# First block's mixers: the fourth scan output and the gate products of RWKV stand ahead of GLA's levels 5 and 6 on TensorE, not behind them

## Reference

```
# GLA: gated linear attention with a decay per key column (4 heads, key 32, value 64)
scores[i, j] = sum_k q[i, k] * k[j, k] * exp(cum[i, k] - cum[j, k])     for j <= i
out = scores @ v + (q * exp(cum)) @ state
out = rms_norm(out) * silu(gate)

# RWKV7 (4 heads of 64), token by token
sa    = -state @ kk
state = state * w + sa (kk * a)^T + v k^T
out   = state @ r
y     = (group_norm(out) + bonus) * (sigmoid(g_lr) @ g2)
```

## Time and profile before

| | us |
|---|---|
| median of 3 runs | 2974.25 |
| lowest and highest | 2971.95, 2977.4 |
| the profiled execution, its own time | 2977.13 |
| its span, first to last instruction | 2975.3 |
| PE busy in the span | 2775.5 (93%) |
| DVE busy | 1543.2 (52%) |
| ACT busy | 1086.0 (37%) |
| mean granted clock of PE | 0.952 |

### The profile page before, as it was taken

How to read it: one execution, slowest core, us unless ns; L and a number is a source line. 1 busy time by engine, 2 the same in 40 slices (tenths; PEclk the granted TensorE clock), 3 DMA queues, 4 the chain that set the end, 5 groups by cost and what they waited for, 6 DMA issues and landing times. The chain is left out here.

```text
span 2975.3 us, 38798 instructions
## 1 busy us (share of the span) xinstructions
PE 2775.5 (93%) x14972; PEld 2386.3 (80%) x14972; DVE 1543.2 (52%) x2136; ACT 1086.0 (37%) x1524; POOL 208.2 (7%) x205
## 2 busy tenths in 40 slices
PE   7999999999999999969999999949999997899999
PEld 5778888888877798858988888848888775788887
DVE  3526675233355366647777777773232525742433
ACT  2434223222233242235555565532232416531222
POOL 0011200000000122050000000110000002000000
PEclk9998889999999999979999999979999996899999
DMA  4210024143222100248888888954242120251521
GB/s 152 90 62 1 29 71 124 50 138 85 85 83 90 45 1 29 86 123 235 250 237 234 228 236 235 271 144 113 60 135 85 54 64 20 85 142 50 149 69 66
DMA packets 435566, 335.25 MB, mean 113 GB/s; under 512 B 23488, under 2 KB 375744, under 8 KB 435312
## 3 DMA queue, kind: packets, MB, share of 16 engines
q1 hardware_dynamic: 429360, 318.14, 37.2%
q0 software_dynamic: 3008, 10.09, 1.0%
q10 hardware_dynamic: 3072, 5.24, 0.5%
HBM read 323.43 MB, written 9.99 MB: 112 GB/s over the span
## 5 line engine op out<-in xcount | busy, mean ns | idle before, releaser
L2506 PE MATMUL psum<-x_split,gate_up_split 128*128 128x512 f32 x1024 | 399.2, 390 | 2.1 <-PEq L2715 2.1
L2507 PE MATMUL psum<-x_split,gate_up_split 128*128 128x512 f32 x1024 | 399.0, 390 | 0.0
L2508 PE MATMUL psum<-x_split,gate_up_split 128*128 128x512 f32 x1024 | 398.9, 390 | 0.0
L3586 PE MATMUL psum<-x_slots_split,gate_up_split 128*128 128x320 f32 x1424 | 381.1, 346 | 16.4 <-DVE gate_up_split L3807 12.9
L3587 PE MATMUL psum<-x_slots_split,gate_up_split 128*128 128x160 f32 x1424 | 315.9, 242 | 0.0
L2634 DVE TENSOR_TENSOR arena<-arena,psum 128x512 f32<-128x512 f32 x66 | 45.4, 688 | 488.1 <-ACT arena L2572 488.1
L2847 PE MATMUL psum<-x_split,w_split 128*128 128x512 f32 x1152 | 271.9, 395 | 12.0 <-DVE w_split L2884 6.8
L3586 PEld LDWEIGHTS psum<-x_slots_split,gate_up_split 128*128 128x128 f32 x1424 | 262.6, 190 | 24.6 <-issue 22.6
L2847 PEld LDWEIGHTS psum<-x_split,w_split 128*128 128x128 f32 x1152 | 217.0, 190 | 66.6 <-issue 14.5
L3587 PEld LDWEIGHTS psum<-x_slots_split,gate_up_split 128*128 128x128 f32 x1424 | 266.1, 192 | 1.9
L2572 ACT ACTIVATE arena<-psum 128x512 f32<-128x512 f32 x66 | 39.6, 601 | 594.9 <-PE psum L2508 594.9
(11 more groups left out here) (520 smaller groups left out, 4790.2 us busy)
## 6 DMA issues: line engine op xcount, KB each, us to landing
arena<-in_moe_w_gate SPq DMA_DIRECT2D x91, 512.0 KB, 4.2
arena<-in_moe_w_up SPq DMA_DIRECT2D x91, 512.0 KB, 5.6
arena<-in_moe_w_down SPq DMA_DIRECT2D x176, 256.0 KB, 5.1
arena<-in_ffn_w_gu SPq DMA_DIRECT2D x88, 512.0 KB, 5.3
arena<-in_w_in SPq DMA_DIRECT2D x32, 1024.0 KB, 5.2
arena<-in_ffn_w_down SPq DMA_DIRECT2D x108, 256.0 KB, 5.2
arena<-in_ffn_w_gate SPq DMA_DIRECT2D x22, 512.0 KB, 4.1
arena<-in_ffn_w_up SPq DMA_DIRECT2D x22, 512.0 KB, 5.6
```

The source lines that it names most:

```text
L2506: nc.tensor.matmul(out, w[0], XR[:, 0, k, :], start=k == 0, stop=False)
L2507: nc.tensor.matmul(out, w[0], XR[:, 1, k, :], start=False, stop=False)
L2508: mm = nc.tensor.matmul(out, w[1], XR[:, 0, k, :], start=False, stop=k == DT - 1)
L3586: hi = lambda start, stop: nc.tensor.matmul(out, wt[0], XE[:, k8, :, :].rearrange("p s n -> p (s n)"), start=start, stop=stop)
```

## The change

In PE's list of `stage_mixers`, `R.pe_scan_out(3)` and `R.pe_gate()` move ahead of `L.pe_level(5)`. Before, the fourth scan output stood between the levels 5 and 6 and the gate behind level 6. No list of another engine changes, no instruction is added or removed, and both layers run the new order.

```diff
@@ -3088,10 +3088,10 @@
                 R.pe_scan_state(2)
                 R.pe_scan_out(2)
                 R.pe_scan_sa(3)
+                R.pe_scan_out(3)
+                R.pe_gate()
                 L.pe_level(5)
-                R.pe_scan_out(3)
                 L.pe_level(6)
-                R.pe_gate()
                 L.pe_diagonal()
                 L.pe_turn()
                 L.pe_out(0)
```

## The result

The changed kernel takes 2991.03 us (median of 6 runs, 2983.51 to 2996.39), the kernel before in the same measurement 2973.46 (6 runs, 2966.74 to 2982.11): a ratio of 1.0054, 95% interval 1.0037 to 1.0072, so 17.6 us slower by the medians. The forecast was 2992.7, slower. Two later measurements of the same two kernels, further down, gave 1.0087 (1.0056 to 1.0118) and 1.0080 (1.0062 to 1.0098). The profiled execution took 2996.39 us, its span is 2994.6, and the mean granted clock is 0.952 as before.

A forecast was written before the change was run, and what follows sets the result against it. PE sets the pace up to the first state, with DVE only 1.08 and 0.40 us from doing so. 14.6 us of delay plus 3.8 of clock gives 18.4, so 2974.25 + 18.4 = 2992.7 us; range 2985 to 2999.5.

The forecast's parts named there:

- The chain: Both layers' mixers: RWKV's work on PE covers GLA's levels and updates; moved ahead, it delays level 5 by about 8.2 us.
- the wait ahead of the scan output: PE, ahead of the fourth scan output: a new idle of about 0.7 us for the fourth `sa` row from DVE.
- the wait ahead of level 6: PE, between levels 5 and 6: idle of about 2.5 us for update 5, where the scan output stood.
- DVE's idle before update 5: DVE, ahead of update 5: about 8 us with nothing to do, waiting for level 5's matmuls.
- The sum at full clock: Fourth `sa` matmuls to DVE's copy of the first state: 6.99 us longer in the first layer, 7.65 in the second, 14.6 together.
- a term put at nothing: Beside the delayed levels: ACT's take of levels 5 and 6, POOL's diagonal and the earlier ACT weight piece cost 0 us.
- The clock: Levels 5 and 6 behind the gate: one level of each layer at half clock, 3.8 us, bounds 0 to 7.6.
- rival A: Both levels in both layers stay at full clock: 14.6 us slower, 2988.9 us; chance 0.22.
- The rule of the Trainium skill: Clock falls come from long PE waits: level 5 at full clock, level 6 slow only if its idle suffices; 14.6 to 18.4 us.
- B: Both levels of both layers run at half clock: 22.2 us slower, 2996.4 us; chance 0.22.
- C: Low clock moves off the stretch behind the first state, 4.4 us back per layer: net 5.8, 2980.1 us; chance 0.06.
- Rival D: The order makes no difference, as something ending later covers the chain: 2974 us; chance 0.02.

The follow-up runs named there:

- out_first: Kernel before with only the fourth scan output moved ahead of level 5, the gate left behind level 6, both layers; ratio 1.0033 to the kernel before.
- small_pool: Changed kernel with GLA's diagonal product on POOL cut to 4 of each head's 64 columns; one time, 2996.14 us.

## Why the prediction was right

**The chain.** The levels are one chain between PE and DVE, and RWKV's work was its cover. Right in each step: the wait ahead of the scan output (0.7 forecast, 0.61), level 5 behind the gate (7.53 + 1.17 = 8.70 us behind `sa` forecast for the second layer, 8.93 measured), the wait ahead of level 6 (2.5, 2.31), DVE's idle before update 5 (about 8, 8.66), PE's wait for the first state (about 3, 3.07 to 3.21), no idle before L377.

**The sum at full clock.** 6.99 + 7.65 = 14.6 was forecast for D and 7.87 + 8.55 = 16.4 measured. The 0.9 missing in each layer is for the most part a term put at nothing ("I cost it, POOL's diagonal and the earlier ACT weight piece at nothing"): "It starts 8.07 later than now, so update 6 ends at 388.64 + 8.07" kept update 6 at 2.22 us, but it now meets POOL's diagonal and takes 2.82. The same meeting costs the weight piece 0.41 and gives HGRN's gate 0.41 back. The remaining 0.3 are small: the wait, the gate and the levels are each 0.05 to 0.13 longer.

**The clock.** This is the step that failed: "I take one level of each layer, 3.8: the gate's fall is seen in both layers". In the first profile of the changed kernel both levels of both layers ran at full clock (1.99 us each), as rival A had it, and the reason given does not hold: a second profile of the unchanged kernel has the whole gate in the second layer and no fall for 6.15 us behind it, and with three quarters of the gate gone the clock falls all the same. Half clock on a level does occur: the whole of out_first's level 6, and a part of level 6 in the first layer of two further profiles of the changed kernel (0.65 and 0.81 us) and of small_pool (0.78), each behind the 2.31 us of idle and none on level 5. The term had the right sign; on D it was worth ((24.84 - 24.42) + (24.99 - 24.42)) / 3 = 0.3 us on average, not 3.8. That the total of 18.4 lies near the measured 17.6 is therefore luck: 3.5 us too much for the levels' clock stand against two things left out, the 1.8 us above and 2.4 us of clock lost behind D (19.1 us to the last product against 16.7 on D, on average), and outside the mixers the profiles of the two kernels differ by 6.8 us one way and 7.9 the other, of which the sum had nothing. The later measurements, 26 and 24 us by their ratios, lie at the upper end of the forecast range, which reached to 2999.5 - 2974.25 = 25.3 over the kernel before, one just outside it and one inside. What they hold beyond 19.1 is not explained; the 34 us are a candidate.

**The rule of the Trainium skill.** "TensorE: Matmul & The Clock Gate", section "Loop structure matters more than you think", puts the fall down to waits. By it the prediction had level 5 at full clock and level 6 in doubt, and that is what came: every slow level 6 stood behind an idle of 2.31 us (five of the thirteen that did, over all runs), and level 5 was never slow. But the fall with no wait ahead of it remains against it.

**The other rivals.** B asked for half clock on both levels, and no profile has it. C asked for the tail's stretch at full clock; it is at 0.50 for 8.78 us as before. Rival D, that the order makes no difference, fell with the wait for L377, 3 us in place of 0.20. Of what was put at nothing, ACT's takes, its earlier weight piece and the transfers show no wait behind them; POOL's diagonal does.

## What to carry to other kernels

Where a chain goes back and forth between two engines, independent work on one of them is worth its place between the links, not its own duration: moved ahead as a block it delays the whole chain by its length and leaves every link uncovered. Read the slack of the engine that comes after the chain (here 1.08 and 0.40 us) before moving anything, and check which operations of a third engine the delayed step will now meet. When single times scatter by more than the effect, a distance between two instructions inside the stage decides with a few profiles what the timed runs only hint at, for that stage alone.

## What was not expected of the hardware

- PE at half clock while it is busy without a break: 34.10 us of 34.10 at 0.50, in a stretch of mostly 64-column matmuls on 128 rows.
- DVE's multiplications with inputs in SBUF take 0.3 to 0.4 us longer beside a POOL instruction that reads SBUF (1.76 to 2.06 for four, 0.42 to 0.72, 2.29 to 2.70), and not when that instruction handles 16 columns in place of 256. POOL's four instructions then still fill 3.35 us, but 2.26 of them are one that started inside the weight piece and waited for its end.
- The same kernel's profiles differ by 8.6 us over 130 us of the second layer (129.6 and 138.2 from L1200 to the fourth `sa`, kernel before), with 4.0 and 23.9 us of it at half clock.
- Behind the same gate, in the same order, the clock fell 0.3 to 1.0 us after the start of the diagonal (L557) in five mixers of the kernel before, and stayed full for 6.15 us in the sixth.
